# Forgetting attention's value products of two heads on the two column halves of TensorE, with each finished row block copied and turned back

## What is computed

```
logits = q @ k.T * scale + F[t] - F[s]        # s <= t, row blocks of 128
p = softmax(logits)
o = p @ v                                      # per head, 64 columns
...
o = concat([rmsnorm(o_fox, g_fox), rmsnorm(o_sb, g_sb)])
x = x + o @ w_out
```

## Time and profile before

| | us |
|---|---|
| median of 3 runs | 1654.25 (1651.65 to 1654.41) |
| profiled execution | 1652.9 |
| its span from first to last instruction | 1650.7 |
| TensorE busy | 1618.8 (98% of the span) |
| VectorE, ScalarE, GpSimd busy | 886.8, 637.3, 236.7 |
| DMA | 141.59 MB, mean 86 GB/s |

### The profile page before, as it was taken

How to read it: one execution, slowest core, us unless ns; L and a number is a source line. 1 busy time by engine, 2 the same in 40 slices (tenths; PEclk the granted TensorE clock), 3 DMA queues, 4 the chain that set the end, 5 groups by cost and what they waited for, 6 DMA issues and landing times.

```text
span 1650.7 us, 19212 instructions
## 1 busy us (share of the span) xinstructions
PE 1618.8 (98%) x7582; PEld 1278.0 (77%) x7582; DVE 886.8 (54%) x1449; ACT 637.3 (39%) x1089; POOL 236.7 (14%) x216
## 2 busy tenths in 40 slices
PE   7999999999999999999999999999999999999998
PEld 5566788876767888888888887786788888888887
DVE  6566456665476455334343324577554677777332
ACT  4332224446555333223322222466563344444222
POOL 1223202400021234110110203000013300000000
PEclk9999999999999999999999999999999999999999
DMA  7121113221211332333332322421103222232322
GB/s 254 48 65 51 51 44 103 89 77 52 65 51 52 128 93 87 102 102 91 101 97 95 103 89 72 159 71 39 52 1 102 87 85 98 90 102 89 127 90 77
DMA packets 39493, 141.59 MB, mean 86 GB/s; under 512 B 4355, under 2 KB 5123, under 8 KB 39084
## 3 DMA queue, kind: packets, MB, share of 16 engines
q1 hardware_dynamic: 39404, 140.37, 26.7%
HBM read 138.24 MB, written 2.11 MB: 85 GB/s over the span
## 4 chain that ended last, share of the span: by engine, by line
PE 88%; DVE 4%; POOL 3%; ACT 2%; issue 1%; DMA 1%; SPq 0%; POOLq 0%; ACTq 0%; DVEq 0%
PE ps L402 85%; PE ps L405 3%; POOL sqs L2123 2%; POOL sqt L2121 1%; DVE wlo L901 1%; ACT whi L1539 1%; DMA wraw<-in_ws 0%; DMA x<-in_x 0%; DVE uT L1066 0%; DVE olo L1318 0%; DVE uT L1064 0%; ACT ohi L1834 0%; PE ps L887 0%; ACT PT L1859 0%; DVE raw L1115 0%
## 5 line engine op out<-in xcount | busy, mean ns | idle before, releaser
L901 DVE TENSOR_TENSOR wlo<-wraw,whi 128x1024 fp32r<-128x1024 f32 (+2 forms) x244 | 304.2, 1251 | 453.0 <-ACT whi L1539 452.5
L402 PE MATMUL ps<-hThi,whi 128*128 128x512 f32 x1128 | 455.6, 404 | 3.0 <-DVE sqT L1430 1.1
L402 PE MATMUL ps<-hThi,wlo 128*128 128x512 f32 x1128 | 440.3, 390 | 0.0
L402 PE MATMUL ps<-hTlo,whi 128*128 128x512 f32 x1128 | 440.0, 390 | 0.0
L1539 ACT ACTIVATE whi<-wraw 128x1024 fp32r<-128x1024 f32 (+2 forms) x244 | 252.2, 1038 | 480.4 <-PE ps L402 455.5
L402 PEld LDWEIGHTS ps<-hThi,whi 128*128 128x128 f32 x1128 | 212.3, 188 | 62.1 <-issue 21.5
L402 PEld LDWEIGHTS ps<-hThi,wlo 128*128 128x128 f32 x1128 | 212.0, 188 | 45.2
L402 PEld LDWEIGHTS ps<-hTlo,whi 128*128 128x128 f32 x1128 | 212.4, 188 | 44.5 <-issue 3.6
L402 PE MATMUL ps<-whi,hThi 128*128 128x512 f32 (+1 forms) x224 | 86.7, 387 | 0.0
L402 PE MATMUL ps<-whi,hTlo 128*128 128x512 f32 (+1 forms) x224 | 84.1, 376 | 0.0
L402 PE MATMUL ps<-wlo,hThi 128*128 128x512 f32 (+1 forms) x224 | 83.9, 375 | 0.0
(11 more groups left out here) (307 smaller groups left out, 2436.2 us busy)
## 6 DMA issues: line engine op xcount, KB each, us to landing
wraw<-in_ws SPq DMA_DIRECT2D x236, 512.0 KB, 3.5
x<-in_x SPq DMA_DIRECT2D x4, 512.0 KB, 5.2
x<-in_x SPq DMA_DIRECT2D x1, 2048.0 KB, 8.6
Fb<-forget_rows SPq DMA_DIRECT2D x1, 2048.0 KB, 7.1
out<-ys SPq DMA_DIRECT2D x8, 256.0 KB, 2.4
dec<-in_dec SPq DMA_DIRECT2D x1, 1024.0 KB, 14.4
wraw<-in_ws SPq DMA_DIRECT2D x4, 256.0 KB, 2.6
vec<-in_vec SPq DMA_DIRECT2D x1, 650.0 KB, 10.9
```

The costliest lines, as they stand in the source:

```text
L402: return t.matmul(o, l, r, start=first, stop=last)
L901: v.tensor_tensor(wlo[h][:, 0:width(i)], wraw[h][:, 0:width(i)], whi[h][:, 0:width(i)].bitcast(F32), ALU.subtract).then_inc(lo_done[h], 1)
```

## The change

- values(u) does both heads of a pair: weights are 64 columns of fv, moving is the 128x128 piece of PTf, outputs go to partitions 0 to 63 and 64 to 127 of the bank, so that the row block lies there transposed (features by queries). It waits for both evacs of the pair and runs at even steps as values(u-6).
- TensorE's order within a step becomes turn(u-3), out_norm_turn, back, values(u-6), scores(u).
- After a row block's last pair ScalarE copies the bank to W5 (heads_out, at steps 18, 20, 34, 36), and TensorE turns it back with four transposes into the bank (back, at 19, 21, 35 and one after the output projection's first slot, into bank 1). VectorE's shares then wait for x_bk; the square follows as finished(q).
- The steps at which out_norm_turn, out_norm_high, out_norm_low and out_norm_scale stand move by one where needed.

```diff
--- before.py
+++ after.py
@@ -341,8 +341,8 @@
     s_mk = sem("s_mk")
     s_qk, s_z, s_ab, s_ln, s_sc, s_sum, s_tr, s_ev, s_pv = (
         sem(n) for n in ("s_qk", "s_z", "s_ab", "s_ln", "s_sc", "s_sum", "s_tr", "s_ev", "s_pv"))
-    x_qk, x_mx, x_ex, x_tr, x_ea, x_ev, x_pv, x_nv = (
-        sem(n) for n in ("x_qk", "x_mx", "x_ex", "x_tr", "x_ea", "x_ev", "x_pv", "x_nv"))
+    x_qk, x_mx, x_ex, x_tr, x_ea, x_ev, x_pv, x_bk, x_nv = (
+        sem(n) for n in ("x_qk", "x_mx", "x_ex", "x_tr", "x_ea", "x_ev", "x_pv", "x_bk", "x_nv"))
     o_c, o_sq, o_sc, o_tr, o_hi, o_lo = (sem(n) for n in ("o_c", "o_sq", "o_sc", "o_tr", "o_hi", "o_lo"))
     w_y, w_r, w_0, w_1 = (sem(n) for n in ("w_y", "w_r", "w_0", "w_1"))
 
@@ -784,31 +784,48 @@
                 free[b] = [(x_ea if u % 2 else x_ev, u // 2 + 1)]
 
             def values(u):
+
                 n, h = pairs[u]
                 b = 6 if n > 1 else 7
-                w.wait_ge(x_ea if u % 2 else x_ev, u // 2 + 1)
+                w.wait_ge(x_ev, u // 2 + 1)
+                w.wait_ge(x_ea, u // 2 + 1)
                 w.wait_ge(fv_c, 4)
                 if h == 0:
                     take(b)
                 for k in range(n + 1):
-                    op = mm(ps[b][:, h * 64:(h + 1) * 64], PTf[u % 4][:, k * 128:(k + 1) * 128], fv[:, k, h * 64:(h + 1) * 64],
-                            k == 0, k == n)
-                op.then_inc(x_pv, 1)
-                if h == 7:
-                    free[b] = [(x_nv, 2 * (13, 15, 29, 31).index(u) + 2)]
+                    for i in range(2):
+                        op = mm(ps[b][64 * i:64 * i + 64, h * 64:h * 64 + 128], fv[:, k, (h + i) * 64:(h + i + 1) * 64],
+                                PTf[(u + i) % 4][:, k * 128:(k + 1) * 128], k == 0, k == n)
+                        if k == n:
+                            op.then_inc(x_pv, 1)
+                if u == 30:
+                    free[b] = [(o_c, 8)]
+
+            def back(q, b):
+
+                w.wait_ge(o_c, 5 + q)
+                if b == 1:
+                    take(b)
+                for k in range(4):
+                    op = across(b, k, W5[q % 3][:, k * 128:(k + 1) * 128])
+                op.then_inc(x_bk, 1)
+                free[b] = [(x_nv, 2 * q + 2)]
 
             for u in range(38):
                 while u == 3 and not fox_go:
                     yield
+                if 3 <= u < 35:
+                    turn(u - 3)
+                if u in (7, 23, 27):
+                    out_norm_turn({7: 3, 23: 4, 27: 5}[u], 3)
+                if u in (19, 21, 35):
+                    back((19, 21, 35).index(u), 7 if u == 21 else 6)
+                if u >= 6 and u % 2 == 0:
+                    values(u - 6)
                 if u < 32 and u % 2 == 0:
                     scores(u)
-                if 3 <= u < 35:
-                    turn(u - 3)
-                if u in (7, 22, 26):
-                    out_norm_turn({7: 3, 22: 4, 26: 5}[u], 3)
-                if 5 <= u < 37:
-                    values(u - 5)
-                yield
+                yield
+            flow.later(1, lambda: back(3, 1))
             flow.later(1, lambda: out_norm_turn(6, 3))
             flow.later(2, lambda: out_norm_turn(7, 3))
 
@@ -1393,13 +1410,13 @@
 
             def shares(q, n):
                 u = (13, 15, 29, 31)[q]
-                c, b = 48 + 8 * n, 6 if n > 1 else 7
+                c, b = 48 + 8 * n, (6, 7, 6, 1)[q]
                 w.wait_ge(x_ex, u + 1)
                 if q:
                     w.wait_ge(x_nv, 2 * q)
                 v.reciprocal(st2[:, 40:48], st2[:, c:c + 8]).then_inc(x_nv, 1)
                 w.wait_ge(x_nv, 2 * q + 1)
-                w.wait_ge(x_pv, u + 1)
+                w.wait_ge(x_bk, q + 1)
                 w.wait_ge(o_sc, 3 * (4 + q))
                 w.wait_ge(o_sq, 4 + q)
                 v.tensor_tensor(heads(W5[3][:], 8), heads(ps[b][:], 8), st2[:, 40:48].unsqueeze(2).to_broadcast([128, 8, 64]),
@@ -1414,12 +1431,13 @@
                     evac(u - 3)
                 if u == 8:
                     out_norm_low(3, 0, "gsb", 3)
-                if u in (23, 27):
-                    out_norm_low(4 + u // 27, 4, "gfox", 3)
-                if u - 5 in (13, 15, 29, 31):
-                    q = (13, 15, 29, 31).index(u - 5)
-                    shares(q, (3, 0, 2, 1)[q])
-                yield
+                if u in (24, 28):
+                    out_norm_low(4 + u // 28, 4, "gfox", 3)
+                if u in (19, 21, 35):
+                    q = (19, 21, 35).index(u)
+                    shares(q, (3, 0, 2)[q])
+                yield
+            flow.later(1, lambda: shares(3, 1))
             flow.later(1, lambda: out_norm_low(6, 4, "gfox", 3))
             flow.later(2, lambda: out_norm_low(7, 4, "gfox", 3))
 
@@ -1895,6 +1913,17 @@
                     w.wait_ge(x_pv, u - 3)
                 a.activation(PTf[u % 4][:, 0:wd], ps[4 + u % 2][:, 0:wd], ACT.Copy).then_inc(x_ea, 1)
 
+            def heads_out(q, u):
+
+                w.wait_ge(x_pv, u + 1)
+                if q == 3:
+                    w.wait_ge(x_bk, 1)
+                a.activation(W5[q % 3][:], ps[7 if q % 2 else 6][:], ACT.Copy).then_inc(o_c, 1)
+
+            def finished(q):
+                w.wait_ge(x_nv, 2 * q + 2)
+                out_norm_square(4 + q)
+
             for u in range(38):
                 while u == 3 and not fox_go:
                     yield
@@ -1904,14 +1933,15 @@
                     evac(u - 3)
                 if u == 7:
                     out_norm_high(3, 0, "gsb", 3)
-                if u in (22, 26):
-                    out_norm_high(4 + u // 26, 4, "gfox", 3)
-                if u - 5 in (13, 15, 29, 31):
-                    q = (13, 15, 29, 31).index(u - 5)
-                    w.wait_ge(x_nv, 2 * q + 2)
-                    out_norm_square(4 + q)
+                if u in (23, 27):
+                    out_norm_high(4 + u // 27, 4, "gfox", 3)
+                if u in (18, 20, 34, 36):
+                    heads_out((18, 20, 34, 36).index(u), u - 5)
+                if u in (19, 21, 35):
+                    finished((19, 21, 35).index(u))
                 yield
             flow.later(1, lambda: out_norm_high(6, 4, "gfox", 3))
+            flow.later(1, lambda: finished(3))
             flow.later(2, lambda: out_norm_high(7, 4, "gfox", 3))
 
         none = lambda b, p, done: None
@@ -2162,8 +2192,8 @@
             for u in range(38):
                 while u == 3 and not fox_go:
                     yield
-                if u in (5, 20, 24, 36):
-                    out_norm_scale({5: 3, 20: 4, 24: 5, 36: 6}[u])
+                if u in (5, 21, 25, 37):
+                    out_norm_scale({5: 3, 21: 4, 25: 5, 37: 6}[u])
                 yield
             flow.later(1, lambda: out_norm_scale(7))
```

## The result

The changed kernel takes 1680.25 us (median, 1677.21 to 1682.66) against 1653.2: 1.0161 of the time before, 95% interval 1.0146 to 1.0176, or +27 us. The forecast was slower by 17, 1671 and at most 1677: the sign came out and so did the loop of waits; the size did not.

What follows compares the result with a forecast made beforehand. TensorE was taken to bound the stage only because scores run ahead; scores last makes a serial loop, 59.6 us for 42.7, with back(3) +17.3, giving 1671 us (chance 0.83), range 1664 to 1677.

Steps and rivals of the forecast that it cites:

- the loop of waits: Forgetting attention: scores(u-2), lowest, shares, odd evac, turn, values, scores(u) become one serial loop; its price is 17.3 us.
- the drain: Forgetting attention after the last projection block, steps from u = 3, 1191.85 to 1234.58 us; forecast to take some 59 us.
- Half-periods A and B: Loop stretches after n = 3 scores (4.17 us) and n = 0 scores (3.45 us); together 7.62 against 5.40 before.
- the sum: From turn(0) to the first projection matmul: 59.6 us against 42.7, +16.9, and back(3) makes +17.3.
- out_norm_turns are hidden in the wait: The out_norm_turns at 7, 23 and 27, 0.45 us each, fit the wait ahead of the odd turn and cost nothing.
- The clock falls: Rival: waiting TensorE drops to 1.2 GHz, its loop terms double at most; up to 1702, 1686 if half hit; chance 0.05.
- one of its own signs of being wrong: The prediction counted itself wrong if the granted clock was below 1.00 in the stretch of attention after the last projection block.
- the entry: TensorE's switch into the column halves ahead of a pair's values: 0.07 us taken, unknown range 0.07 to 0.14.
- the other choice of the prediction: If switching into the halves drained TensorE like the exit, 0.14 us instead of 0.07, the sum would be 1.1 us more.
- The way from the column halves straight to the scores' row halves: TensorE's switch from values to scores, shown by no row: 0.14 us taken, bounds nothing and twice that.
- TensorE's bare sum: TensorE's work alone, -8.0 for values plus switching and 1.8 for back(): -4.4 us; as a rival 1648.5, chance 0.04.
- back() waits: TensorE's three waits for heads_out copies queued on ScalarE behind shares and evac: together 4.9 us.

Runs made afterwards that it cites:

- fillers: Changed kernel plus 48 unused matmuls ahead of the odd turn, into the score bank free in that step, at even steps 6 to 30: 1673.64 us, ratio 1.0123.
- scores first: Changed kernel with scores(u) back at the head of TensorE's step; halves, copies and back() stay: 1655.82 us, ratio 1.0011.
- The halves alone: Changed kernel without heads_out and back(), attention output not the reference's: 1652.13 us with scores at the step's head, 1652.16 with scores last and evac ahead of shares.
- the last such experiment: Changed kernel without heads_out and back(), scores last on TensorE, evac ahead of shares on ScalarE: 1652.16 us, ratio 0.9996.
- copies first, heads_out too: Changed kernel with ScalarE's order turned to evac, heads_out, shares; TensorE's order unchanged: 1653.67 us, ratio 1.0002.

## Why the prediction was right or wrong

**Right: what bounds.** TensorE looked like the bound of the drain, and the argument was that it is so only because scores run ahead. Putting scores last in the kernel before cost 15 us without any other change, a part of which is again the clock.

**Right: the loop, its place and its size.** Half-periods A and B came out at 4.22 and 3.49 us for 4.17 and 3.45, the waits stand ahead of the odd turns and are put down to ScalarE's PTf copy, and cutting the loop at either of two engines gave back 24 us. With the clock held by fillers the changed kernel takes 20.7 us more than the one before; without the 3.2 that the fillers cost themselves that is 17.5 against the 17.3 of the sum, and the drain 59.9 against 59.6. That out_norm_turns are hidden in the wait held too.

**Wrong: the clock's term, put at nothing.** The step of the prediction that failed is this one: the sum goes by the full clock throughout, and *The clock falls* was a rival with chance 0.05, left out of the range. That the granted clock is below 1.00 in the drain was one of its own signs of being wrong, and it showed. The mean clock was under that of the kernel before in all eight runs (0.986 to 0.993); in the first profile 31 of the 70 us were at 1.2 GHz, which cost 10 us and took the time from some 1671 to 1680. I had drawn a loop in which TensorE waits for 2.9 of every 7.6 us (the text says nearly half; by its own terms it is under 40%), and the full clock that I read in the earlier trace rows was that of a TensorE that never waits: no row showed it at such a load. That should have been a case with a high chance, next to the loop and not against it. The price itself was right: TensorE's 4.1 us of a period doubled make 4.1 lost of 11.7, or 10.8 for 31 us at the lower level, and 10 were measured; the rest of the period is the other engines', and ScalarE's copy takes 0.58 us at either clock. What was missing is how much of the drain would be hit, and no run gives a rule for that. The Trainium skill, "TensorE: Matmul & The Clock Gate", Why this matters for your kernels, tells to leave no long gap between bursts of matmuls. The gaps of this trace are shorter than those that the page warns of, 2.0 us at the most, and the clock fell all the same.

**Wrong, small: the entry.** I took 0.07 us into the halves from three transposes; four transposes show 0.11 (1205.60 to 1206.16 with scores first). Here the other choice of the prediction was nearer: the Trainium skill, "TensorEngine Tiling (Array Packing)", Key Properties, has every change of mode drain the engine. With 0.14 as for the exit that asked for 1.1 us more; the row gives 16 x 0.04 = 0.6. The way from the column halves straight to the scores' row halves, for which no row stood, cost the 0.14 that I took (1206.88 to 1207.90 is 16 x 0.055 + 0.14).

**Wrong in the alternative, not in the forecast: TensorE's bare sum.** It promised -4.4 us if nothing waited. Without a loop the kernels came out between -0.3 and +3.4 us. In "scores first" TensorE pays entry, exit and an entry into the row halves as well (1206.53 to 1206.79, one transpose and 0.15 of change), and back()'s waits come on top. The halves alone are worth 0.7 to 0.8 us (1.8 in the drain of the last such experiment) and not 6.2: "if nothing waits" was the term that failed, and there seven waits of turns for their banks cost 3.5 us.

**Right in kind: back() waits.** 4.9 us were forecast for three; the waits shown are 3.6 at the matmul and 4.4 at the weight load.

## What to carry to other kernels

When an instruction is moved behind others in one engine's queue, follow its result through the other engines' queues and back: if anything between the old and the new place waits for something queued behind that result's consumer, the two have become one loop, and its length is the sum of all answers, however idle the engines are. The repair can be on another engine (here two lines swapped on ScalarE were worth 24 us, the clock included). If the sum itself leaves TensorE waiting again and again, as here for up to 2 us in every half-period of 4, put the lower clock into the forecast. And when work that nothing uses is put into gaps, look for the wait that it is to fill: behind it, it is in the way.

## What the hardware showed

- In the first profile of the changed kernel the granted clock fell to 0.50 four times in the drain, at 1198.7, 1215.8, 1236.2 and 1246.5 us. In the 5 us before each, TensorE was busy for 3.0 to 3.5 us, and its longest gap in the drain was 2.0 us. No rule follows: 1253 to 1258 were busy for 3.1 us at 1.00. How much of the drain was hit differs from run to run (mean clock 0.986 to 0.993), and the same program swings by 9 us with it. Work that nothing uses, put for the most part in the gaps, made the kernel 9.5 us faster.
- At half clock the sixteen value matmuls of a pair took 1.98 us instead of 1.09, while the wait ahead of them still was 1.53 us, since ScalarE's part takes the same time: 31 us at the lower level cost 10.
- The clock fell outside the drain too: in "copies first, heads_out too" it was 0.83 in the mean from 35 to 45 us, at 0.998 for the whole run. On that chip the kernel before takes 1654.9 in its runs at 0.998 and 1652.6 in those above; that it is the same place there isn't shown, but 2 us between two runs of one kernel are nothing that an experiment did.
- A change between the full array and column halves cost 0.11 us going in and 0.14 coming out. For a pair of heads of 64 columns that makes 1.13 us against 1.68 for n = 3, but 0.48 (1209.82 to 1210.75, less four transposes at 0.112) against 0.42 for n = 0: there the two changes cost more than the halves save.
